# Who makes the low parts of split weights: VectorE alone in place of VectorE and GpSimd

## The reference

```python
def hybrid_layer(x, ...):                      # run twice
    h = rms_norm(x, g_mix_pre)
    z = h @ w_in                                # 1024 -> 2816
    rq, rk, rv, rg, aq, ak, av, gu, gv = split(z)
    y = concat(silu(rg) * retention(rope(rq), rope(rk), rv),
               dilated_attention(rope(aq), rope(ak), av),
               spatial_gating(gelu(gu), gelu(gv), w_s, b_s))
    x = x + rms_norm(y @ w_out, g_mix_post)
    h = rms_norm(x, g_ffn_pre)
    gate, up = split(h @ w_gate_up)             # 1024 -> 2 x 2816
    return x + rms_norm((silu(gate) * up) @ w_down, g_ffn_post)

def second_block(x, c, ctx, ...):
    shift, scale, ... = split(silu(c) @ w_ada + b_ada)     # six parts of 1024
    h = x * (1 + scale) + shift
    z, xbc, dt, u, gates = split(h @ w_in_2)
    xs, bm, cm = split(silu(conv5(xbc)))        # 2048, 512, 512 channels
    y = scan(xs, dt, bm, cm, forward, start from ctx) \
      + flip(scan(flip(...), start from ctx)) + xs * d_skip
    y_a = rms_norm(y * silu(z)) * g
    y_p = pooled(u) @ pool_w                     # windows of 2, 4, 8, 16
    g_a, g_p = split(sigmoid(gates + b_gate))
    merged = g_a * (y_a @ w_branch_a) + g_p * (y_p @ w_branch_b)
    x = layer_norm(alpha * x + gate1 * (merged @ w_out_2))
    h = x * (1 + scale2) + shift2
    # 32 experts, the best 2 of one group for each token
    return layer_norm(alpha * x + gate2 * moe(h))
```

## Time and profile before

| | before |
|---|---|
| median of 3 runs | 1611.19 us (1610.83 to 1612.89) |
| the profiled execution | 1614.68 us, span of its instructions 1612.8 us |
| PE busy | 1566.7 us, 97% of the span |
| DVE busy | 783.9 us, 49% |
| ACT busy | 612.4 us, 38% |
| POOL busy | 480.6 us, 30% |
| granted TensorE clock, mean | 0.995 |
| low parts made by DVE / by POOL | 151 / 142 |

### The profile page before, as it was taken

One profiled execution on the slowest core, in us unless ns is written; L12 is line 12 of the kernel. 1 busy time (PEld: TensorE's weight loads), 2 busy tenths in 40 slices (PEclk: granted clock), 3 DMA queues, 4 the chain that ended last, 5 costly groups with the idle time before them and its releaser, 6 DMA issues.

```text
span 1612.8 us, 24052 instructions
## 1 busy us (share of the span) xinstructions
PE 1566.7 (97%) x9726; PEld 1182.5 (73%) x9726; DVE 783.9 (49%) x1291; ACT 612.4 (38%) x1110; POOL 480.6 (30%) x318
## 2 busy tenths in 40 slices
PE   7999999999999999999999999999999999999987
PEld 6889899868889998888787888998644444444442
DVE  5654434246564332479767776446433333233223
ACT  4653444345553443455446665332211111111110
POOL 4432655434334544300126665353300000000000
PEclk9999999999999999999999999999999999999999
DMA  8644996537439986443427666957899999999994
GB/s 284 213 157 131 256 268 223 180 96 271 143 87 304 263 261 222 141 105 105 130 53 221 198 192 204 301 141 293 353 405 425 420 422 424 422 422 424 421 422 179
DMA packets 249972, 410.50 MB, mean 255 GB/s; under 512 B 7685, under 2 KB 196689, under 8 KB 228480
## 3 DMA queue, kind: packets, MB, share of 16 engines
q1 hardware_dynamic: 242864, 379.09, 67.7%
q10 hardware_dynamic: 3584, 19.86, 3.1%
q0 software_dynamic: 3408, 9.95, 1.7%
HBM read 407.72 MB, written 1.15 MB: 254 GB/s over the span
## 4 chain that ended last, share of the span: by engine, by line
PE 86%; DMA 6%; DVE 3%; issue 1%; POOL 1%; ACT 1%; SPq 0%; ACTq 0%; DVEq 0%; POOLq 0%
PE ps L144 84%; DMA arena<-in_w_expert_gate 2%; DMA arena<-in_w_expert_up 2%; PE ps L146 2%; DVE arena L154 1%; DVE arena L150 1%; DMA ring<-in_w_out 1%; POOL split_r L150 1%; DMA ring<-in_w_gate_up 1%; ACT split_r L148 1%; DVE split_r L150 1%; DMA rows<-in_b_s 0%; POOL arena_r L150 0%; ACT arena L148 0%; DVE arena_r L150 0%
## 5 line engine op out<-in xcount | busy, mean ns | idle before, releaser
L144 PE MATMUL ps<-arena_r,split_r 128*128 128x256 f32 (+1 forms) x2984 | 460.1, 288 | 2.6 <-POOL split_r L150 2.6
L150 POOL TENSOR_TENSOR split_r<-ring,split_r 128x1024 fp32r<-128x1024 f32 (+1 forms) x142 | 328.8, 2317 | 276.0 <-ACT split_r L148 247.0
L144 PEld LDWEIGHTS ps<-arena_r,split_r 128*128 128x128 f32 x2984 | 393.4, 188 | 23.2 <-issue 17.1
L148 ACT ACTIVATE split_r<-ring 128x1024 fp32r<-128x1024 f32 (+1 forms) x293 | 295.9, 1020 | 253.0 <-PE ps L144 183.6
L150 DVE TENSOR_TENSOR split_r<-ring,split_r 128x1024 fp32r<-128x1024 f32 (+1 forms) x151 | 225.8, 1497 | 290.6 <-ACT split_r L148 290.4
L144 PE MATMUL ps<-split_r,arena_r 128*128 128x512 f32 (+1 forms) x1520 | 340.8, 378 | 7.6 <-issue 3.1
L144 PEld LDWEIGHTS ps<-split_r,arena_r 128*128 128x128 f32 x1520 | 276.0, 189 | 54.4 <-issue 12.1
L144 PE MATMUL ps<-arena 128*64 128x512 f32 (+8 forms) x1232 | 303.3, 471 | 4.6 <-DVE arena L160 3.7
L144 PE MATMUL ps<-ring,arena 128*64 128x512 f32 (+2 forms) x688 | 226.1, 575 | 2.6 <-DMA rows<-in_w_expert_gate 0.9
L144 PE MATMUL ps<-hhh_r,split_r 128*128 128x256 f32 (+1 forms) x976 | 228.5, 322 | 0.0
L144 PEld LDWEIGHTS ps<-arena 128*64 128x64 f32 (+2 forms) x1232 | 120.9, 150 | 114.2 <-issue 101.2
(11 more groups left out here) (160 smaller groups left out, 1299.2 us busy)
## 6 DMA issues: line engine op xcount, KB each, us to landing
ring<-in_w_gate_up SPq DMA_DIRECT2D x88, 512.0 KB, 7.4
ring<-in_w_in SPq DMA_DIRECT2D x57, 512.0 KB, 5.4
arena<-in_w_ada SPq DMA_DIRECT2D x24, 1024.0 KB, 7.4
arena<-in_w_expert_gate SPq DMA_DIRECT2D x12, 2048.0 KB, 26.1
ring<-in_w_down SPq DMA_DIRECT2D x22, 1024.0 KB, 4.8
ring<-in_w_expert_up SPq DMA_DIRECT2D x11, 2048.0 KB, 25.1
ring<-in_w_expert_down SPq DMA_DIRECT2D x11, 2048.0 KB, 26.9
ring<-in_w_in SPq DMA_DIRECT2D x28, 768.0 KB, 5.9
```

The costliest lines, as they stand in the source:

```text
L144: made = e.matmul(*a, **k)
L148: made = e.activation(*a, **k)
L150: made = e.tensor_tensor(*a, **k)
```

## The change

`by_vector` returns true for every quarter. All 293 low parts are made by DVE; POOL makes none. Nothing else is edited: the streams of PE, ACT and SP hold the same instructions as before, and PE waits for a count on DVE's semaphore where it waited for one on POOL's.

```diff
         def by_vector(n):
 
-            for l in range(2):
-                if first["out", l][1] <= n < first["up", l, 0][1]:
-                    return True
-                if first["z", l, 1][1] <= n < first["down", l][1] + 22:
-                    return n % 2 == 0
-            if n_quarters1 <= n < first["merged",][1]:
-                return True
-            return n % 2 == 0 and n >= first["u",][1]
+            return True
```

## The result

The changed kernel takes 1614.76 us in the median of 20 runs (1613.11 to 1617.22); the kernel before, in 20 runs beside it, 1612.28 us. The ratio is 1.0014, 95% interval 1.0008 to 1.0020: slower by 2.3 us (2.5 between the medians), and above the range that I gave, which ended at 1613.0. The forecast was 3.25 us faster.

The account below looks back on a forecast made before the run. PE was taken as the bound, busy 1566.7 of 1612.8 us, so only its 46 us of standing still could move. Terms -2.9 + 1.9 - 1.05 - 1.2 = -3.25 took the median 1611.19 to 1607.9 us, range 1604.8 to 1613.0.

Parts of the forecast that it names:

- point 4: Loops of z, up and down, and conv: 0, the added DVE lows covered by a lead of three quarters.
- Point 3: Change of layers: -2.9 us (bounds -4 to -1.5), from two PE waits shortened by 1.48 and 1.45.
- Point 5: Start of the scan: +1.9 us (+1.1 to +3), a low part now ahead of weights_of(1) and meeting POOL's sums.
- Point 6: Inside the scan: 0 (bounds 0 to +7), DVE's queue holds at 92 to 95% busy.
- rival C: Scan becomes bound by DVE, stopped by POOL's sums and squares: up to +7 there, total 1615 us; chance 0.13.
- Point 1: Start of z, layer 0: 0 (bounds -1 to +1), extra lows take up the saved stall and idle time.
- Point 2: Start of up: 0 (bounds -1.5 to +1), an earlier low in layer 0 offset by later modulation weights.
- Points 7 and 8: PE's waits on POOL's lows shrink: u and branch_a -1.05 us (-1.08 to 0), out2 -1.2 (-1.87 to 0).
- Point 9: Experts: 0, and earlier gains carry through 1:1, since each transfer is issued when PE releases a buffer.
- rival B: Experts' transfers swallow the end's gain, or the layer change gives less: 1609.4 to 1610.2 us; chance 0.17.

Follow-up runs that it names:

- one_low: Kernel before, with only two subtractions moved from POOL to DVE, the low part of quarter 25 of stage z in each layer: 1621.18 us, ratio 1.0055.
- two_back: Changed kernel, with the low part of quarter 25 of stage z in each layer back on POOL: 1608.14 us, ratio to before 0.9969.
- att_first: Changed kernel; in steps 18, 22 and 26 of stage z DVE's attention-block subtraction stands ahead of the weights' low part: 1607.87 us, ratio to before 0.9969.
- tail_dve: Kernel before, with only POOL's 20 low parts of u, branch_a, branch_b and out2 moved to DVE: 1609.94 us, ratio 0.9977.
- best: The run both, with DVE's four low parts in stage up behind the second norm_low and the fourth at the layer change behind norm_low: 1600.51 us, ratio 0.9921.
- scan_late: Changed kernel; on DVE in the scan each step's low part stands behind weights_of, not ahead of it: 1612.29 us, ratio to before 0.9996.
- both: Changed kernel with the two changes of order of att_first and scan_late together: 1603.54 us, ratio to before 0.9945.

## Why the prediction was wrong

- **The step that failed is point 4**, "Loops of z, up and down, and conv: 0 ... each low is made three quarters ahead of use". The lead covers those who wait for the low part. It says nothing of those who wait for what stands behind it on DVE. A low part three quarters ahead of use is, by the four places of `split_r`, one that can start only when PE is done with the quarter before the present one, so it is never ready long ahead. With POOL's parts gone every step of DVE in these loops holds such a low part, not every other one; where PE's next input is in the same step, the wait is PE's. I counted DVE's busy share (66.5 of 179 us), which doesn't show this. One_low prices the point at +8.8 us where I had 0, more than all gains, and two_back and att_first take 6.6 and 6.9 of it back.
- **The clock** was in no term. I wrote that the change can only move the 46 us in which PE stands still, and took each wait at its own length. In the changed kernel's trace a stretch at half clock behind 2.35 to 3.07 us of standing still cost 1.4 to 1.7 more, and it counts as busy time of PE. The same may have made the tail worth more than -2.25 (tail_dve: -2.9 by the medians; no run separates the two).
- **Point 3** held: -1.6 and -1.5 in the trace for -1.48 and -1.45; by itself -2.4 in the times for -2.9.
- **Point 5** held to 0.1: wait 3.07 for about 3.1, the low part stretched to 1.87 by POOL's sum; its clock was missing.
- **Point 6** held, and rival C fell: DVE was busy 119.2 of 130 us in 860 to 990, PE had no gap but the first wait (126.93 + 3.07 = 130), and DVE's low parts took 1.24 on average.
- **Point 1** was mis-sized: the gain is -1.8 in the trace and -2.4 in the times, beyond my bound of -1. I had let the extra low parts take up what the stall at 40.44 gave back. But a DVE operation just ahead of them, which had taken 1.69 us, took 0.19 without POOL's low parts beside it, so DVE began its four at 20.90, not 22.61, and was done with them at the same time as before.
- **Point 2** held: wait 1.60 for 1.49, and in best, where norm_low stands ahead of the four low parts, it is gone.
- **Points 7 and 8**: in this trace the waits of 0.63 and 1.87 went entirely, 0.45 became 0.28, and with the clock the step was -4.5 in the profiles, -2.9 in the times. The kernel before has its half clock there in this execution; its other executions differ in mean clock. The wait at out2 isn't gone for good: with all low parts on DVE too, scan_late's trace has 2.21 there (PE at 1119.75) and both's 0.70, each for DVE's low part, and in scan_late that low part and its high part ran right behind a transfer of 6.44 us.
- **Point 9** held: tail_dve, both and best brought their gains to the end, and rival B's swallowing did not show.

Lines of the changed kernel for points 6 and 3: DVE's group in the scan, then DVE and PE at the change of layers.

```profile
L150 DVE TENSOR_TENSOR split_r<-ring,split_r 128x1024 fp32r<-128x1024 f32 x30 | 37.2, 1240 | 3.4 <-ACT split_r L148 3.4
```

```profile
357.07 3.57 DVE L150 TENSOR_TENSOR split_r<-ring,split_r 128x768 fp32r<-128x768 f32 x4
360.55 1.29 DVE L150 TENSOR_TENSOR arena_r<-arena,arena_r 128x512 fp32r<-128x512 f32 x2
361.88 0.69 DVE L158 CUSTOM_DVE_ANT_0 arena<-X 128x512 f32<-128x512 f32 x1
...
361.99 1.30 PE L144 MATMUL ps<-split_r,arena_r 128*128 128x384 f32 x6 [1.08 <-DVE arena_r L150]
```

## What to carry to other kernels

When an instruction that waits is moved to another engine's queue, list what stands behind it in that queue and who waits for that; its own length and the engine's busy share don't show the price. Work that only becomes possible at the last moment (a ring of few places) belongs behind everything in its step that another engine waits for. And a new wait of TensorE of some 2 to 3 us may cost more than its length through the clock: in the changed kernel's trace 2.35 us cost 3.9 and 3.07 cost about 4.5, and in two other traces (one_low, two_back) waits as long had no such stretch behind them.

## What the runs showed of the hardware

- Behind PE's waits of 2.35, 2.35 and 3.07 us the granted clock was 0.72 over 6 us; with the first two filled by products of zeros it was 1.00. It was also 1.00 behind waits of 2.59 at 361 and of 1.87 at 44 in the kernel before, behind 2.35 in layer 1 of one_low and behind 3.06 in two_back, while tail_dve has 0.72 behind its 2.59 and one_low 0.72 behind 2.18 at 44. The length of the wait alone doesn't decide; what does stays open.
- A low part of 128x1024 took DVE 1.562 us on average before and 1.243 when POOL's were gone, one of 128x768 1.157 and 0.954: 142 more instructions cost DVE 90 us of busy time.
